# Moving TensorE's announcement of the jump back within the large expert bodies

## What is computed

```python
logits = (t @ router_w).astype(jnp.float32) + router_b
...
for e in range(N_EXPERTS):
    hid = jax.nn.silu(t @ w_gate[e]) * (t @ w_up[e])
    y = y + combine[:, e:e + 1] * (hid @ w_down[e])
```

## Time and profile before

| | |
|---|---|
| median of 3 runs | 1769.99 us (1769.48 to 1770.95) |
| the profiled execution | 1768.32 us |
| its span in the profile | 1766.6 us |
| TensorE busy | 1514.4 us, 86% |
| instructions in the span | 27607 |
| mean DMA rate | 356 GB/s |
| mean granted TensorE clock | 0.93 |

### The profile page before, as it was taken

The page is one execution under the profiler, slowest core; times in us unless marked ns, Lnnn a source line. Parts: engine busy times, 40 slices in busy tenths (PEclk is TensorE's granted clock), DMA queues, the critical chain, the costliest instruction groups (busy, mean ns, idle before and its releaser), DMA issues.

```text
span 1766.6 us, 27607 instructions
## 1 busy us (share of the span) xinstructions
PE 1514.4 (86%) x12032; PEld 1003.2 (57%) x12032; DVE 584.4 (33%) x1096; ACT 188.5 (11%) x455; POOL 361.5 (20%) x161
## 2 busy tenths in 40 slices
PE   7799999999999999987699955798976656898567
PEld 6578788888888878653444522433434324335223
DVE  0453657877576243431111211112011110212013
ACT  0001012200011100041100100100101001001002
POOL 0006730178677777300000000000000000000000
PEclk9899999999999999988899988898998888899789
DMA  9997896678778754549997899998999999999996
GB/s 386 425 426 222 344 393 256 244 328 361 314 312 346 285 211 176 233 153 426 426 411 280 332 428 425 427 423 373 389 426 426 427 427 426 421 416 416 426 427 260
DMA packets 50348, 629.54 MB, mean 356 GB/s; under 512 B 5699, under 2 KB 8164, under 8 KB 11264
## 3 DMA queue, kind: packets, MB, share of 16 engines
q1 hardware_dynamic: 48904, 621.58, 84.9%
q10 hardware_dynamic: 1272, 5.54, 0.8%
HBM read 623.43 MB, written 3.67 MB: 355 GB/s over the span
## 4 chain that ended last, share of the span: by engine, by line
PE 65%; DMA 29%; DVE 2%; issue 2%; POOL 1%; SPq 1%; ACT 0%; DVEq 0%; POOLq 0%
PE bank L1639 23%; PE bank L917 15%; DMA ring<-in_w_up_gate 10%; PE bank L1401 9%; DMA ring<-in_w_down 7%; PE bank L946 6%; DMA region_g<-in_w_up_gate 5%; PE bank L1477 4%; DMA region_g<-in_w_down 4%; PE bank L886 2%; DMA ring<-in_ada_w 2%; PE bank L958 2%; DMA ring<-in_w_in 1%; POOL ring L771 1%; PE bank L953 1%
## 5 line engine op out<-in xcount | busy, mean ns | idle before, releaser
L771 POOL TENSOR_TENSOR ring<-ring 128x1024 f32<-128x1024 f32 x152 | 359.0, 2388 | 329.6 <-DMA ring<-in_w_in 226.2
L917 PE MATMUL bank<-ring,region_b 128*32 128x256 f32 (+1 forms) x3104 | 307.4, 478 | 123.9 <-DMA ring<-in_w_up_gate 97.4
L917 PEld LDWEIGHTS bank<-ring,region_b 128*32 128x32 f32 (+1 forms) x3104 | 129.8, 129 | 282.6 <-issue 141.7
L946 PE MATMUL bank<-ring,region_f 128*32 128x256 f32 (+1 forms) x1920 | 174.9, 458 | 53.2 <-DMA ring<-in_w_down 53.1
L1639 PE MATMUL bank<-ring,region_a 128*128 128x256 f32 x768 | 171.4, 380 | 2.3 <-DVE region_e L2402 1.8
L1639 PE MATMUL bank<-ring,region_x 128*128 128x256 f32 x768 | 170.4, 379 | 0.9 <-issue 0.7
L1639 PEld LDWEIGHTS bank<-ring,region_a 128*128 128x128 f32 x768 | 145.3, 190 | 25.0 <-issue 4.8
L1639 PEld LDWEIGHTS bank<-ring,region_x 128*128 128x128 f32 x768 | 145.3, 190 | 21.1 <-issue 1.1
L946 PEld LDWEIGHTS bank<-ring,region_f 128*32 128x32 f32 (+1 forms) x1920 | 72.6, 124 | 139.8 <-issue 69.3
L2715 DVE TENSOR_TENSOR work<-work,bank 128x128 f32<-128x128 f32 (+1 forms) x32 | 10.3, 321 | 425.7 <-ACT work L1899 425.7
L2204 DVE SCALAR_TENSOR_TENSOR bank<-ring,condT,bank 128x512 f32<-128x512 f32 x192 | 144.9, 755 | 5.8
(11 more groups left out here) (262 smaller groups left out, 1297.8 us busy)
## 6 DMA issues: line engine op xcount, KB each, us to landing
ring<-in_w_up_gate SPq DMA_DIRECT2D x111, 2048.0 KB, 29.3
ring<-in_w_down SPq DMA_DIRECT2D x56, 2048.0 KB, 21.6
ring<-in_ada_w SPq DMA_DIRECT2D x44, 2048.0 KB, 11.9
ring<-in_w_in SPq DMA_DIRECT2D x31, 2048.0 KB, 13.9
region_g<-in_w_up_gate SPq DMA_DIRECT2D x16, 2048.0 KB, 25.6
ring<-in_w_branch SPq DMA_DIRECT2D x8, 2048.0 KB, 14.9
ring<-in_w_out SPq DMA_DIRECT2D x8, 2048.0 KB, 10.4
region_g<-in_w_down SPq DMA_DIRECT2D x8, 2048.0 KB, 31.6
```

Source lines behind the costliest of these rows:

```text
L771: ins = pool.tensor_tensor(quarter(s, *out)[:, k:k + 4, :], quarter(s, *in0)[:, k:k + 4, :], quarter(s, *in1)[:, k:k + 4, :], op)
L917: last = nc.tensor.matmul(bank_of(x, j)[n * c:n * c + n, 0:2 * m], tokens(x, 8 * half + k), w[:, k % 4, :, m * c:m * c + m], start=(half = ...
L946: last = nc.tensor.matmul(bank_of(x, q)[n * c:n * c + n, 0:m], hidT[x][:, k, :], w[:, k % 4, m * c:m * c + m], start=(k == 0), stop=(k == ...
```

## The change

The announcement of the jump back moves down within the large bodies: from behind down product 0 to directly ahead of the last four steps of down product 1. It is the same instruction, once per large body; small bodies, the announcements at lines 849, 1325 and 1766, and all other engines stay as they are.

```diff
@@ -1364,7 +1364,6 @@
             if len(xs) == 2:
                 extra("add E")(2)
 
-            announced = pe.mark_branch_hint_location() if base == WIDE else None
             if ends:
                 end_of_last()
                 for x in EXTRA:
@@ -1383,6 +1382,7 @@
             if not xs:
                 add_up(0)
             loaded_half(5, 1)
+            announced = pe.mark_branch_hint_location() if base == WIDE else None
             down(base, 1, last).then_inc(y_full, 1)
             if xs:
                 add_up(0)
```

## The result

The changed kernel is **slower by 0.68%**: 1780.85 us (median of 13 runs, 1770.42 to 1792.85) against 1768.88 us (13 runs of the kernel before beside them, 1766.07 to 1771.8), ratio 1.0068, 95% interval 1.0052 to 1.0083. I had forecast 1770.0 us, within 0.2% of before. Not only the median rose: the runs of one and the same program now lie 22 us apart, against 6 us before.

The account below looks back on a forecast made before the run. Weight loads by the DMA engines bound the expert stage. Instruction 0, gain 0, three jumps in time 0, (1, 3) 1.3 us late but covered 0: sum 0, so 1770.0 us, range 1768.0 to 1773.0, to 1776.5 with lost in flight.

Parts of the forecast that it names:

- What bounds the kernel, and which losses count: Expert stage follows the weight load; TensorE's losses reach the end behind (0, 2) and (1, 2), not (1, 3) and (3, 0).
- the cover: Behind (1, 3) and (3, 0), queued loads keep DMA engines busy; in (3, 0) a 5.9 us loss counts 0 to 2.
- The gap in SP's issues that I named: Behind (1, 3), SP issued nothing between 1292.8 and 1298.5 us, a 5.7 us gap that the queued loads bridged.
- The instruction costs nothing, and nothing can be gained: Four announcements of 31 to 40 ns, as before: 0; jumps back at 0.32 to 0.43 us have no fetch to save.
- Leads: Time from new announcement to jump back: 7.9 us in (0, 2), 8.0 in (1, 2), 5.2 in (1, 3), 8.0 in (3, 0).
- 6.5 us from announcement to a cheap jump: Time a late announcement needs, from (1, 3), between 4.1 and 7.2 us; three jumps in time, (1, 3) 1.3 short but covered.
- the prediction's 1.3 us for that: Time added from the end of a code packet to the end of TensorE's stall, read behind (1, 3).
- the 8 us that the prediction named as a sign of being wrong: The forecast is wrong if the fetch following a late announcement takes over 8 us.
- The reading of the regular fetch: The in-line fetch now brings the jump's target; announced behind it, in the last piece, the announcement starts its own fetch.
- Lost in flight: Announcement meeting a code fetch under way is dropped, in (1, 2) or (3, 0): 5.9 us, 1775.9 up to 1778; chance 0.09.
- Ignored altogether: Late announcement does nothing, all four jumps back fetch on demand: 13.8 us more, 1783.8 us; chance 0.06.
- Carries nothing: Announcement has no effect at either place; jumps back are cheap for another reason: 1770.0 us; chance 0.04.

Follow-up runs that it names:

- four shifted ones: Changed kernel with TensorE's large code, announcement and jump together, moved against its code pieces by LARGE_SLOT 30, 140, 10 or 180 for 80: 1778.06, 1778.59, 1784.49, 1784.11 us.
- the kernel with the later jump: Changed kernel whose bodies with one extra group, (1, 2) and (3, 0), hold up the jump back by a wait and ten idle matmuls: 1794.64 us.
- the three with part of the marks: Kernel before with announcements left out in (1, 3), then (0, 2), then (1, 2) with (3, 0): 1771.58, 1774.81, 1779.55 us.
- 140: Changed kernel with LARGE_SLOT 140 for 80, placing TensorE's large code 60 instructions later against the pieces: 1778.59 us, ratio to before 1.0064.
- 180: Changed kernel with LARGE_SLOT 180 for 80, placing TensorE's large code 100 instructions later against the pieces: 1784.11 us, ratio to before 1.0087.
- 30: Changed kernel with LARGE_SLOT 30 for 80, placing TensorE's large code 50 instructions earlier against the pieces: 1778.06 us, ratio to before 1.0048.
- 10: Changed kernel with LARGE_SLOT 10 for 80, placing TensorE's large code 70 instructions earlier against the pieces: 1784.49 us, ratio to before 1.0089.

## Why the prediction was wrong, step by step

**What bounds the kernel, and which losses count: mostly right.** TensorE's standstill behind (0, 2) reaches the end in full: 4.9 us more at the jump, 6.2 us (3.9 to 8.3) in the time. Behind (1, 3) about two thirds are covered. **Behind (3, 0) the cover was mis-sized.** I took 0 to 2 of 5.9 us; the share of 0.03 right behind it in the changed kernel and the run without the announcements of (1, 2) and (3, 0) show nearly the whole. I had judged by the mean of 1.01 over 500 us, which says that the DMA engines are busy there, not for how long the queue would last. The gap in SP's issues that I named was that of (1, 3).

**The instruction costs nothing, and nothing can be gained: right.** Moved by less, to 13.6 us and more ahead of the jump, it gives 0.9998.

**Leads: wrong, and without consequence.** I read them off the matmul group of line 946. An announcement is executed by the sequencer, and that ran 1.0 to 4.5 us ahead. The row of the announcement before, 1274.7 us, should have been set beside its matmuls first. Three of the true leads, 9.0 to 9.3 us, are larger than mine, and these three jumps were the dear ones.

**"6.5 us from announcement to a cheap jump": this is the step that failed.** It came from one case, the announcement of (1, 3) at 1274.7 us, with 4.1 and 7.2 us as its ends. What the runs showed for the delay from announcement to the start of the 16 KB packet, in the changed kernel's three executions:

```
expert   delay us, three executions            jump back ns
(0, 2)   none up to the jump at 9.0; 7.0; 6.8   5574;  476;  416
(1, 2)   none up to the jump, three times       6500; 6274; 6142
(1, 3)   3.6; 3.6; 4.0                           422;  338;  431
(3, 0)   none up to the jump at 9.3, twice; 7.3 5382; 5383;  642
```

The packet in (3, 0) that I take for the regular one, 0.5 to 0.9 us behind each announcement, is not counted.

From the start of the packet until a jump can end another 2.4 us go by, the packet of 1 us and 1.4 us to resume; the prediction's 1.3 us for that was close. The case that I had taken was of the one expert that is quick in all three. Over all 30 jumps back with 8.9 to 9.9 us of lead (three executions of the changed kernel, four shifted ones, and the two jumps that were not held up in the kernel with the later jump: 0.41 us in (0, 2), 5.84 in (1, 3)) the delay was 1.0 to 11.0 us where a packet can be told as its own, and 16 jumps were cheap, under 0.7 us. In the two that were held up it reached 14.9 us. That is what stands in place of my 6.5, and over the 8 us that the prediction named as a sign of being wrong. On the other side, every announcement with 13.6 us or more of lead gave a cheap jump, 16 of 16, in the kernel before, in the one with the mark four steps earlier and in the three with part of the marks. The upper end of 7.2 us had no ground: it was the price of an unannounced jump, a request that TensorE stands waiting for, and says nothing of one made ahead. The 9.8 us in (1, 2) of the kernel before (announced at 1204.4, packet at 1214.2 us) are no second case against the 6.5: that packet stays in its place when the announcement moves. Taken for a delay, they would have given the right outcome in (1, 2) by luck.

**The reading of the regular fetch: borne out as far as the traces reach.** That the announcement of the kernel before is served by the fetch in line fits the packets of (1, 2) and (3, 0), which stay in place when the announcement moves or is left out. That a late announcement finds that fetch spent and needs one of its own fits too: where it is late and works, a packet of its own follows the regular one, in (0, 2) and (3, 0) of the changed kernel and in (0, 2) with the mark four steps earlier. What a packet holds no trace shows. The mechanism was right as far as it can be seen; the time that a fetch of its own takes was not.

**The rivals.** "Lost in flight" gave 1775.9 to 1778 us, nearer to the result than my forecast, but (0, 2) with the mark four steps earlier and (3, 0) in the third execution, if its first packet is the regular one, are announcements with a fetch under way that worked, and (0, 2), which it had as cheap, was dear in the profiled execution. "Ignored altogether", 1783.8 us, is near the slow half of the runs, but (1, 3) is cheap in all three executions, and without any announcement it is 1788.54. Its price per jump, 5.9 us, was right (4.9 to 6.3 measured); it lacked that a dear jump back in (1, 2) makes the unannounced onward jump cheaper by 2 to 3 us. "Carries nothing" falls with the run without announcements: 19.1 us. The Trainium skill ("Runtime: NRT & Kernel Launch", section "Instruction fetch mechanics") calls the fetch ahead purely sequential, with a stall for a taken branch whose target is not there. Without the instruction this case's runs agree (5.8 to 6.2 us, four times); with it, early enough, they do not (0.32 to 0.43 us). The gain did not come: nothing behind the late announcement was spared.

**Which way it went, put together.** The sum should have been: each jump back has some chance of being dear, at 6 us in (0, 2), 5 to 7 in (3, 0), 2 to 4 net in (1, 2), 2 in (1, 3). At all four that is 15 to 19 us, where the runs gave 18.0 and 19.1; the changed kernel's median lies at 12 of them. How large the chance is no run before the change could say.

**What stays open** is why the delay is 1 us in one place and 15 in another. Three things go with it in the traces; none was tried by itself.

- **The place in the piece.** No sharp rule holds, but place is not out as an influence. In the three executions of the changed kernel and the four shifted ones, an announcement 74 to 160 instructions into the jump's piece gave a cheap jump 12 times in 14, one between 56 ahead of the piece and 26 into it 3 times in 14. (1, 2) was dear in all five near the start of the piece and cheap in both further in (with 140 and 180). The line between the two groups is drawn after the outcomes were known.
- **The expert.** (0, 2) and (1, 3) were cheap 11 times in 14, (1, 2) and (3, 0) 4 times in 14. Expert and place go together too much to be told apart here.
- **The load of the DMA engines.** They were nearly full in slow and in quick cases alike (99.8% and 98.9% in the two fences on the announcements), so load does not tell 3.6 from over 9 us. But all four delays under 3.4 us (1.0 with 30, 1.2 with 10, 1.5 with the later jump and 2.6 with the mark four steps earlier) are in (0, 2), where the engines stood still just before the announcement or behind it. With 30, in the three microseconds ahead of the announcement at 979.8 us, and with the mark four steps earlier, from the announcement at 975.6 us to its packet, the DMA share is 0.00 and 0.02:

```profile
976.80:979.80 3.00, 3.00 (x19) 0.76 (x16) 2.44 (x5) 0.00 (x0) 0.00 (x0) 1.00 0.00 0
...
975.60:978.20 2.60, 2.60 (x28) 1.30 (x26) 1.44 (x3) 0.00 (x0) 0.00 (x0) 1.00 0.02 6
```

Idle engines are not enough: (0, 2) of the changed kernel has the same hole ahead of its announcement, and waited 6.8 us, 7.0 us and over 9.0 us. The other delays of fetches of their own don't spread evenly but lie in four groups: 3.4 to 4.1, 6.8 to 7.3, 10.2 to 11.0 and 13.6 to 14.9 us. What sets these steps is open.

No version here beats the kernel before; the mark ahead of the first four steps equals it, and is the latest place tried that does.

## What to carry to other kernels

Announce a far jump as early as the lead costs nothing: here 13.6 us and more were enough 16 times in 16, and 9 us in 16 of 30, but a delay of 14.9 us was seen as well. An announcement in time is worth 5 to 6 us at the jump, 2 to 6 of them at the end, and the instruction itself costs nothing. A latency that rests on one case is no latency, and the fastest one seen is no bound: ask of every instance in the trace whether the announcement or something else set its time, and where one instance is left, vary it before relying on it. Where runs of one program spread more after a change than before, one trace is one draw, and a theory needs several.

## What the hardware showed that I had not expected

- The delay between an announcement and a 16 KB code fetch of its own runs from 1.0 to 14.9 us, in one program at the same place from 6.8 to over 9.0 us ((0, 2)).
- An unannounced jump back costs 5.2 to 6.6 us: 2.9 to 4.1 us to the packet, about 1 us for it and 1.4 us until the jump ends. Two such jumps in a row are cheaper than their sum: behind a dear jump back the onward one takes 3.9 to 5.1 us, behind a cheap one 6.6 to 7.2.
- Announced 14.0 to 19.9 us ahead, the jumps of (1, 2) and (3, 0) were cheap with no packet of their own: the only one behind the announcement lies 8.2 to 10.1 us ahead of the jump, wherever the announcement stands.
- An announcement that runs while another code fetch is under way was not lost in the three cases where that can be told: (0, 2) with the mark four steps earlier, (3, 0) in the third execution of the changed kernel, and (3, 0) with the later jump, there too late.
- TensorE's sequencer runs 1.0 to 4.5 us ahead of the matmuls next to the announcement, so the time of an announcement is not that of its neighbours.
